# Hybrid decoder layer on one core: `w_ada` loads moved ahead of the `w_in` blocks, states loaded later, group-norm roots by Ln and Exp on ScalarE, query factors made earlier

## The reference

```python
mod = silu(c) @ w_ada + b_ada                      # (9, 6144): sh1, sc1, gt1, sh2, sc2, gt2
h = rmsnorm(x, g_mix) * (1 + sc1) + sh1
z = h @ w_in                                       # 2816 columns: q_a k_a v_a | q_h f_h i_h g_h
q_a, k_a = rotary(q_a), rotary(k_a)
o_a = rmsnorm(sink_attention(q_a, k_a, v_a, ...), g_attn_out)          # window 128, 8 heads, 2 kv heads
f = lb + (1 - lb) * sigmoid(f_h)
o_h, S = hgrn(q_h, 1 - f, i_h, log(f), S0)                             # 4 heads of 128 x 128 state
o_h = rmsnorm(o_h, g_hg_out) * silu(g_h)
x = x + gt1 * (concat(o_a, o_h) @ w_out)
h = rmsnorm(x, g_ffn) * (1 + sc2) + sh2
x = x + gt2 * moe(h)                               # 32 experts, top 4, clamped SwiGLU
y = rmsnorm(x, g_final)
```

## Time and profile before

| what | value |
|---|---|
| time, median of 3 runs (lowest to highest) | 1208.98 us (1208.96 to 1215.12) |
| the profiled execution's own time | 1208.33 us |
| its span, first to last instruction | 1206.5 us |
| TensorE busy, share of the span | 1105.0 us, 92% |
| VectorE busy | 345.3 us, 29% |
| ScalarE busy | 162.0 us, 13% |
| GpSimd busy | 55.6 us, 5% |
| bytes read from memory | 460.30 MB |

### The profile page before, as it was taken

The page is one execution under the profiler, slowest core; times in us unless marked ns, Lnnn a source line. Parts: engine busy times, 40 slices in busy tenths (PEclk is TensorE's granted clock), DMA queues, the critical chain, the costliest instruction groups (busy, mean ns, idle before and its releaser), DMA issues.

```text
span 1206.5 us, 14039 instructions
## 1 busy us (share of the span) xinstructions
PE 1105.0 (92%) x5465; PEld 437.4 (36%) x5465; DVE 345.3 (29%) x761; ACT 162.0 (13%) x312; POOL 55.6 (5%) x86
## 2 busy tenths in 40 slices
PE   6959998899999999999898989898989898989896
PEld 3625575673333333232322323232323232323222
DVE  4213643643223222313131222222222212121214
ACT  3221152131101001000001010001000100000003
POOL 1230001211000000000000000000000000000000
PEclk9988998899999999999999999999999999999999
DMA  9996542669999999999999999999999999999995
GB/s 365 350 353 244 187 161 95 242 235 390 429 429 431 429 432 428 433 431 429 430 432 431 428 431 430 432 430 430 431 431 429 431 430 431 430 430 429 432 429 208
DMA packets 49128, 461.65 MB, mean 383 GB/s; under 512 B 6657, under 2 KB 7873, under 8 KB 22202
## 3 DMA queue, kind: packets, MB, share of 16 engines
q1 hardware_dynamic: 42512, 445.17, 88.2%
q0 software_dynamic: 5600, 13.13, 3.1%
q10 hardware_dynamic: 986, 2.95, 0.7%
HBM read 460.30 MB, written 5.78 MB: 386 GB/s over the span
## 4 chain that ended last, share of the span: by engine, by line
PE 59%; DMA 37%; DVE 3%; issue 1%; POOL 0%; SPq 0%; ACT 0%; DVEq 0%
PE bank L1641 27%; DMA arena<-in_w_up 17%; DMA ring<-in_w_up 14%; PE bank L1521 6%; PE bank L1665 5%; DMA arena<-in_w_down 3%; PE bank L1441 3%; DMA ring<-in_w_ada 2%; PE bank L922 2%; PE bank L1634 2%; PE bank L1101 1%; PE bank L1198 1%; PE bank L946 1%; PE bank L1233 1%; PE bank L1024 1%; PE bank L1182 1%
## 5 line engine op out<-in xcount | busy, mean ns | idle before, releaser
L1641 PE MATMUL bank<-arena 128*64 128x512 f32 x1024 | 240.0, 601 | 11.7 <-DMA arena<-in_w_up 11.1
L1641 PE MATMUL bank<-ring,arena 128*64 128x512 f32 x1024 | 240.0, 601 | 9.6 <-DMA ring<-in_w_up 8.5
L1641 PEld LDWEIGHTS bank<-arena 128*64 128x64 f32 x1024 | 67.3, 136 | 164.6 <-issue 149.4
L1641 PEld LDWEIGHTS bank<-ring,arena 128*64 128x64 f32 x1024 | 66.2, 136 | 162.9 <-issue 137.7
L1665 PE MATMUL bank<-ring,arena 128*64 128x512 f32 x512 | 114.6, 596 | 9.1 <-DMA ring<-in_w_down 9.1
L1665 PE MATMUL bank<-arena 128*64 128x512 f32 x512 | 114.6, 596 | 8.8 <-DMA arena<-in_w_down 8.8
L2217 DVE TENSOR_SCALAR arena<-bank 128x256 f32<-128x256 f32 x64 | 24.2, 420 | 274.3 <-PE bank L1641 274.3
L1521 PE MATMUL bank<-arena,mods 128*128 128x512 f32 (+1 forms) x204 | 93.8, 630 | 0.9 <-DVE arena L2244 0.9
L876 ACT ACTIVATE arena<-arena 128x512 f32<-128x512 f32 x32 | 20.2, 630 | 492.3 <-DVE arena L2217 492.3
L2206 DVE TENSOR_TENSOR x<-x,bank 128x512 f32<-128x512 f32 x64 | 44.0, 688 | 144.3 <-PE bank L1521 144.3
L922 PE MATMUL bank<-const,arena 128*128 128x128 f32 (+3 forms) x348 | 50.3, 285 | 23.0 <-DMA ring<-in_w_down 7.6
(11 more groups left out here) (335 smaller groups left out, 807.0 us busy)
## 6 DMA issues: line engine op xcount, KB each, us to landing
ring<-in_w_up SPq DMA_DIRECT2D x64, 2048.0 KB, 34.0
arena<-in_w_up SPq DMA_DIRECT2D x64, 2048.0 KB, 34.3
ring<-in_w_down SPq DMA_DIRECT2D x32, 2048.0 KB, 33.7
arena<-in_w_down SPq DMA_DIRECT2D x31, 2048.0 KB, 33.4
ring<-in_w_ada SPq DMA_DIRECT2D x16, 1024.0 KB, 8.4
ring<-in_w_ada SPq DMA_DIRECT2D x16, 512.0 KB, 10.9
ring<-in_w_in SPq DMA_DIRECT2D x3, 2048.0 KB, 12.8
ring<-in_w_in SPq DMA_DIRECT2D x5, 1024.0 KB, 12.0
```

The costliest lines, as they stand in the source:

```text
L1641: mm = pe.matmul(B[2 * e + c % 2][64 * a:64 * a + 64, :], lhsT=xTe[:, k, 64 * e:64 * e + 64], rhs=big(PER * s + n)[:, r, 512 * c:512 * (c ...
```

## The change

On SP, ada3 to ada5 are issued ahead of the 2 MB block `Z0 + 5`, and ada6 to ada11 ahead of `Z0 + 7`; all waits on `chunks_used` and `ada_used` in them are as they were. On POOL, the caches, sinks and copies wait for `chunks_used` 13 (the first matmul of attention queries 0) where they followed the states, and the states follow them at `chunks_used` 15 (the first matmul of `inner`). On ACT, the four prompt roots become a logarithm of the mean square each, and three exponentials with scale -0.5 then give the inverse roots at once, so that DVE's four prompt reciprocals go. On DVE, the query factors `qf` and `qkT` are made before the levels, `modT3` is emptied ahead of `take_heads(1)`, the two attention norms become one over 256 tokens, and all norms stand behind `km`. On PE, the router row `cw` is made before `oT`, in another bank, and DVE takes it there.

```diff
@@ SP
             w_in_columns(Z4, 8)
-            w_in_columns(Z0 + 5, 10)
             for i in range(3, 6):
                 w_ada_rows(i)
+            w_in_columns(Z0 + 5, 10)
+            for i in range(6, 12):
+                w_ada_rows(i)
             w_in_columns(Z0 + 7, 12)
-            for i in range(6, 2 * N_ADA):
+            for i in range(12, 2 * N_ADA):
                 w_ada_rows(i)
             w_in_columns(Z0 + 9, 15)
@@ POOL
-            pool.wait_ge(chunks_used, N_ADA + 3)
-            for b in range(NB):
-                pool.dma_start(states[:, b], ...).then_inc(sem("states_full"), 16)
+            pool.wait_ge(chunks_used, Z0 + 5)
             pool.dma_start(vc, ...)
...
+            pool.wait_ge(chunks_used, Z0 + 7)
+            for b in range(NB):
+                pool.dma_start(states[:, b], ...).then_inc(sem("states_full"), 16)
@@ ACT
-            root(r_hg[0], "hs0", heads("hs0"), P)
-            root(r_att[:, P:S], "as1", bank("as1")[:, 0:P], AW)
+            def log_mean(out, name, src, n):
+                wait_filled(act, name)
+                act.activation(out, src, ACT.Ln, scale=1.0 / n, bias=eps).then_inc(emptied(name), 1)
+
+            def inverse_root(ap):
+                act.activation(ap, ap, ACT.Exp, scale=-0.5).then_inc(sem("powers"), 1)
+
+            log_mean(r_hg[0], "hs0", heads("hs0"), P)
+            log_mean(r_att[:, P:S], "as1", bank("as1")[:, 0:P], AW)
...
-            root(r_att[:, 0:P], "as0", bank("as0")[:, 0:P], AW)
-            root(r_hg[1], "hs1", heads("hs1"), P)
+            log_mean(r_att[:, 0:P], "as0", bank("as0")[:, 0:P], AW)
+            log_mean(r_hg[1], "hs1", heads("hs1"), P)
+            for name in ("hs0", "as1", "as0", "hs1"):
+                wait_emptied(act, name)
+            inverse_root(r_hg[0])
+            inverse_root(r_att[:, 0:S])
+            inverse_root(r_hg[1])
@@ PE
+            pe.wait_ge(sem("router_full"), 16)
+            wait_emptied(pe, "modT2")
+            out = take("cw")
+            ...
+            give(mm, "cw")
             out = take("oT")
...
             outer(0, ("ou0", "ou1", "ou2", "ou3"))
-            (the same six lines)
@@ DVE
             first_level()
+            link(dve.memset(flat[:, 3 * P:4 * P], 0.0))
+            dve.tensor_tensor(qf[:, :, 0:NB], qd, fTh, ALU.mult)
+            dve.tensor_tensor(qkT..., qd, kTp[:, :, 0:NB], ALU.mult).then_inc(sem("qf_ready"), 1)
...
+            wait_filled(dve, "modT3")
+            (modT3 to s2T, as it stood further down)
             take_heads(1)
             def norm_heads(t):
-                wait_emptied(dve, f"hs{t}")
-                link(dve.reciprocal(r_hg[t], r_hg[t]))
+                dve.wait_ge(sem("powers"), 2 + t)
...
-            norm_heads(0)
-            norm_values("as1", P, P)
...
             dve.tensor_tensor(km, ...).then_inc(sem("km_ready"), 1)
-            norm_values("as0", 0, P)
+            norm_heads(0)
+            norm_values(0, S)
             norm_heads(1)
-            norm_values("asd", S, NB).then_inc(sem("att_ready"), 1)
+            wait_emptied(dve, "asd")
+            link(dve.reciprocal(r_att[:, S:NTOK], r_att[:, S:NTOK]))
+            norm_values(S, NB).then_inc(sem("att_ready"), 1)
```

More of the change, by code:

```diff
@@ L559, in _ @@
                                    wide(A["b_ada"][0:1, n0:n0 + 512], 0, 9)).then_inc(sem("ada_rows_full"), 16)
-            pool.wait_ge(chunks_used, N_ADA + 3)
-            for b in range(NB):
-                pool.dma_start(states[:, b], A["state_hgrn"][0, b].rearrange("h k v -> k h v")).then_inc(sem("states_full"), 16)
+            pool.wait_ge(chunks_used, Z0 + 5)
             pool.dma_start(vc, A["cache_v_win"][0].rearrange("b s g d -> s b (g d)")).then_inc(sem("cache_full"), 16)
@@ L572, in _ @@
                                A[src][0, :, 1:WIN].rearrange("b s g d -> b (s g d)")).then_inc(sem("rows_stored"), 16)
+            pool.wait_ge(chunks_used, Z0 + 7)
+            for b in range(NB):
+                pool.dma_start(states[:, b], A["state_hgrn"][0, b].rearrange("h k v -> k h v")).then_inc(sem("states_full"), 16)
             wait_emptied(pool, "vt")
@@ L1398, in _ @@
             give(pe.matmul(out[0:64, 0:P], lhsT=C("spread", slice(0, NB)), rhs=vd[0:NB, :], start=True, stop=True), "dvr")
+            pe.wait_ge(sem("router_full"), 16)
+            wait_emptied(pe, "modT2")
+            out = take("cw")
+            for k in range(KT):
+                mm = pe.matmul(out[0:E, 0:1 + NB], lhsT=wr[:, k, :], rhs=sh2T[:, k, :], start=(k == 0), stop=(k == KT - 1))
+            give(mm, "cw")
             out = take("oT")
@@ L1424, in _ @@
             outer(0, ("ou0", "ou1", "ou2", "ou3"))
[L1425 to L1430, removed]
             def project(d):
@@ L1863, in _ @@
             first_level()
+            qd = qh[:, :, S:NTOK]
+            link(dve.memset(flat[:, 3 * P:4 * P], 0.0))
+            dve.tensor_tensor(qf[:, :, 0:NB], qd, fTh, ALU.mult)
+            dve.tensor_tensor(qkT.rearrange("p (h b) -> p h b", h=HH), qd, kTp[:, :, 0:NB], ALU.mult).then_inc(sem("qf_ready"), 1)
             wait_filled(dve, "ada2")
@@ L1949, in _ @@
             link(dve.memset(pbd, 0.0))
[L1951 to L1955, removed]
             def take_heads(t):
@@ L1985, in _ @@
             dve.tensor_copy(by_half(sh2T), cols_of("modT2")[:, 2:4, :, 0:9]).then_inc(emptied("modT2"), 1)
+            wait_filled(dve, "modT3")
+            dve.tensor_copy(by_half(ctmp), cols_of("modT3")[:, 0:2, :, 0:9]).then_inc(emptied("modT3"), 1)
+            wait_emptied(dve, "modT3")
+            link(dve.scalar_tensor_tensor(out=by_half(s2T), in0=by_half(ctmp), scalar=1.0, in1=param(g_ffn_c), op0=ALU.add, op1=ALU.mult))
             take_heads(1)
             def norm_heads(t):
-                wait_emptied(dve, f"hs{t}")
-                link(dve.reciprocal(r_hg[t], r_hg[t]))
+                dve.wait_ge(sem("powers"), 2 + t)
                 wait_emptied(dve, f"hgo{t}")
@@ L1993, in norm_heads, with norm_values @@
                 dve.tensor_tensor(part, part, r_hg[t], ALU.mult).then_inc(sem("hg_ready"), 1)
-            def norm_values(name, lo, n):
-                wait_emptied(dve, name)
-                link(dve.reciprocal(r_att[:, lo:lo + n], r_att[:, lo:lo + n]))
+            def norm_values(lo, n):
                 for j in range(GRP):
@@ L2015, in _ @@
             dve.tensor_tensor(pvr[0:64, :], pvr[0:64, :], bank("dpv")[0:64, 0:P], ALU.add).then_inc(emptied("dpv"), 1)
+            dve.wait_ge(sem("sinks_full"), 16 * 10)
+            wait_filled(dve, "cw")
+            dve.tensor_scalar(cw[0:E, :], bank("cw")[0:E, 0:1 + NB], brout[0:E, :], None, ALU.add).then_inc(emptied("cw"), 1)
+            wait_emptied(dve, "cw")
+            dve.sem_inc(sem("router_row"), 1)
+            dve.tensor_scalar(bdiag[0:E, :], ident[0:E, 0:E], cw[0:E, 0:1], None, ALU.mult).then_inc(sem("router_row"), 1)
             wait_emptied(dve, "qkb")
@@ L2046, in _ @@
             update_states(0, ("ou0", "ou1", "ou2", "ou3"))
[L2047 to L2052, removed]
             def x1_column(d):
```

## The result

| | before | after |
|---|---|---|
| time, median of 4 runs each on one chip (lowest to highest) | 1210.82 us (1208.96 to 1215.12) | 1194.41 us (1191.38 to 1195.86) |
| ratio to before, 95% interval | | 0.9856 [0.9821, 0.9892] |
| the profiled execution's own time | 1208.33 us | 1195.86 us |

The kernel is 16.4 us faster. The forecast was 1184, with a range that ended at 1193: the sign was right, and the time lies 1.4 us above the range.

A forecast was written before the change was run, and what follows sets the result against it. The experts' DMA stream at 430 GB/s has fixed length, so front and tail savings come off in full: 1208.33 less 15.2 (23.5 - 5.4 - 2.9) less 9.5, plus the median's offset, gives 1184 us; range 1174 to 1193.

The forecast's parts named there:

- the new wait at ada12: Front, after attention queries 0 begin: ada12 lands 4.1 to 6.6 us too late behind SP's and POOL's transfers; 5.4 us taken.
- The front waits: PE's four waits for ada chunks before attention queries 0 go, 17.7 us, with 5.8 us of slow running: 23.5 us.
- the close fit: Front: ada6 would land near 71.5 us and PE come to it at 72.7, so no wait was counted.
- slow clock: Front, PE behind ada12's wait: 2.9 us lost, taken from two chunks and the transposes that followed ada3's wait.
- The larger wait: Rival, chance 0.13: SP gets 202 GB/s, the wait at ada12 is 14.5 us, the front gains 6.1; 1193 us.
- The 202: Front: SP's rate in GB/s beside POOL's copies, worked out from `Z0 + 7`'s 2.1 MB in 10.4 us.
- No wait at ada12: Rival, chance 0.22: POOL's small, scattered transfers yield to SP's, so the front keeps 23.5 us; 1175 us.
- The roots: Rival for the tail, chance 0.04: the powers reach DVE after `km`, 3.2 us of removed reciprocals become a wait; 1187 us.
- the table loads' price: ACT in the tail: one load was counted at 1.28 us without drain; the skill adds about 1.38 us per switch.
- The tail: From `od0` to the projection: `km` starts 6.3 us earlier and DVE saves 3.2 us, 9.5 in all (8.8 to 9.9).
- the 1186 with the drains: Time if 2.7 us of drains at two more table switches fell on the path, the tail giving 6.8 us.
- the offset of 0.65: Microseconds by which the median of the runs lay above the profiled execution's 1208.33, added to the sum.

The follow-up runs named there:

- e5: The changed kernel with POOL's old order put back and SP's new order kept; 1198.01 us.
- e8: The changed kernel with each of the two cache copies cut into sixteen parts, same bytes and place in POOL's queue; 1189.76 us.
- e4: The changed kernel with the two cache copies moved behind the states on POOL; 1188.16 us.
- e7: The changed kernel with `Z0 + 7` behind ada14 on SP and the two cache copies behind the states on POOL; 1180.16 us.
- e2: The changed kernel with SP's and POOL's old order put back, ACT, DVE and PE staying new; 1202.59 us.
- e3: The changed kernel with `Z0 + 7` issued behind ada12 on SP instead of ahead of it; 1187.63 us.
- e10: e7 with eleven extra matmuls, whose result nothing uses, on PE ahead of the projection; 1181.85 us.
- e1: The kernel before with only the new order of SP's and POOL's loads; 1204.30 us.
- e6: The changed kernel with `cw` put back behind the first outer products on PE and the first states on DVE; 1192.30 us.

## Why the prediction was wrong

The chain of reasons was right and one term of the sum was too small, the new wait at ada12 with the slow running behind it. By the steps of the prediction:

**The front waits: right.** 23.5 us were forecast; the start of attention queries 0 moved by 23.0 relative to the start of the front, with 0.43 us of wait left at ada6, the close fit.

**The new wait at ada12: the step that failed.** It was to cost 5.4 us and 2.9 of slow clock behind it; it cost 8.83 and 5.2, the whole stretch 14.1 instead of 8.3. Its place and its cause, POOL's transfers beside SP's (e5), were right. Two things were mis-sized. The sum let 8.4 MB go by, ada12 last of them; 10.2 MB went by, since the copies hold up a part of the engines and the rest run ahead into the chunks behind: 2.7 us (e8). In e8 the wait is 6.16 us, inside the 4.1 to 6.6 that the prediction had worked out. The rate was not at fault: 376 GB/s once the transfers ran, between the 360 and 404 taken. And the slow clock was priced by what followed ada3's wait, where short work stood; here a level, a rotation and 32 matmuls of attention queries stand behind it, and they lose 1.7, 0.5 and 2.0 us, with 1.0 for ada12 itself. The size of the wait matters little for this: in e4 a wait of 3.86 still leaves a stretch 8.2 us longer, 4.4 of it slow running.

**The rivals.** The larger wait (1193) is next to the measured time, but its mechanism is not what happened: it put the wait at 14.5 us with SP held to 202 GB/s, and 8.8 were measured. The 202 was misread, too. In the 12.8 us in which `Z0 + 7` landed before the change, SP's queue (q1) moved 3.70 MB and POOL's (q0) 1.02, 370 GB/s in all; only 2.1 of the 3.70 were `Z0 + 7`, and the rest went to the ada chunks issued behind it. So the trace of before already had a load that landed late, beside the same copies, while later ones ran ahead (a window as above, then packets, MB and share of the engines by queue):

```profile
78.40:91.20 12.80, 2.66 (x12) 1.92 (x11) 2.41 (x5) 1.07 (x2) 0.00 (x0) 0.79 0.98 370
...
q1 hardware_dynamic: 1252, 3.70, 74.3%
q0 software_dynamic: 219, 1.02, 24.1%
```

No wait at ada12 (1175) is what e7 makes true by other means, at 1180. The roots are not late: the powers are there 3.6 us before their use. On the table loads' price the Trainium skill ("ScalarE: Activation LUTs", section "What ACT_TABLE_LOAD costs") has a drain with each switch; the exponentials began 1.29 us after their load did (194.66 - 193.37), so these rows again show none.

**The tail: right.** 9.5 us were forecast, `inner` to projection fell by 10.4, a little beyond the upper bound of 9.9, and e2 alone gives 10.0. The attention norm of 256 columns took 1.67 us (1.6 forecast), `cw` in the path 0.6 (1.0 forecast).

**The base of the sum.** The sum went off one profiled execution of 1208.33 us and its median of three, 1208.98; the median of the four runs beside the change is 1210.82, 1.8 above, and the later medians of the same kernel are 1212.0 to 1212.8, 3.0 to 3.8 above. (The rivals' times, and the 1186 with the drains, leave out the offset of 0.65 that the forecast has in.) Part of that is seen at the start. PE's timeline has the same sixteen matmuls of the first stretch at 42.57 us in before, at 46.10 in after and at 42.75 in e8, though nothing of the change lies ahead of them:

```profile
42.57 7.03 PE L1024 MATMUL bank<-ring,arena 128*128 128x512 f32 x16
```

```profile
46.10 7.03 PE L1039 MATMUL bank<-ring,arena 128*128 128x512 f32 x16
```

```profile
42.75 7.03 PE L1039 MATMUL bank<-ring,arena 128*128 128x512 f32 x16
```

Over the twelve profiles of the study this start lies between 42.57 (before) and 46.29 (e3). In after, six transposes at 17.77 us take 1.71 us, which in before took 1.11 at 16.26. The profile on which the sum was made was the earliest of all here, and had the shortest projection but that of e10 (8.78).

Added up: of the 10.4 us between 1184 and 1194.4, ada12 is 5.8, the front waits 0.5, the tail -0.9, and the base 1.8 to 3.8. What is left, 1.2 to 3.2 us, stays open; the slower projection and router of the profiled execution (2.8 of the 3.4 us behind the projection's start) would cover all or most of it, but their times vary from profile to profile in the same way.

## What to carry to other kernels

When loads are moved earlier, ask what else comes to stand beside the next load that is needed, and count what the engines may move before its *last* piece lands: also what is issued behind it, and transfers that load the DMA engines unevenly. The bytes of one transfer over its time to landing aren't its queue's rate when others of the queue were under way beside it. A memory-to-memory copy with a short outermost dimension can be cut into 16 parts at no visible cost, and transfers that nothing waits for belong behind those that something waits for. A sum made off one profiled execution carries that execution's luck; a second profile of the kernel before shows how much that is.

## What the runs showed of the hardware

The slow running behind a wait at ada12 hardly followed the wait's length: behind 3.86, 6.16, 8.41, 8.75 and 8.83 us (e4, e8, e1, e6, after) it cost 4.4, 3.8, 5.3, 4.8 and 5.2 us, each worked out as the stretch less 32.67 and less the wait. In e6 the granted clock was already down to 0.60 in a window in which PE was busy for 95% of the time, with small matmuls. And copies of 0.5 MB that land within 10 to 15 us delayed, by their shape alone, a chunk on another queue by 2.3 to 2.7 us (8.41 to 8.83 less 6.16).
